# Inverting the scans' 64x64 unit triangular blocks on their diagonal 32x32 blocks

## The reference

```python
def gdn_chunked(q, k, v, g, beta, s0):
    cs = GDN_CHUNK                                   # 64
    ...
    tri_strict = jnp.tril(jnp.ones((cs, cs), bool), -1)
    a_mat = jnp.where(tri_strict, jnp.einsum('nbhid,nbhjd->nbhij', kb, kc) * decay, 0.0)
    eye = jnp.eye(cs, dtype=jnp.float32)
    t_mat = lax.linalg.triangular_solve(eye + a_mat, jnp.broadcast_to(eye, a_mat.shape),
                                        left_side=True, lower=True, unit_diagonal=True)
    u = jnp.einsum('nbhij,nbhjd->nbhid', t_mat, vb)
    w = jnp.einsum('nbhij,nbhjd->nbhid', t_mat, kb * jnp.exp(gcum)[..., None])
    ...
```

## Time and profile before

| | us |
|---|---|
| median of 3 runs | 2939.48 |
| profiled execution | 2932.05 |
| its span | 2930.1 |
| PE busy in the span | 2539.1 (87%) |
| VectorE busy | 1476.8 (50%) |
| opener of each inversion | at 551.7, 741.7, 1292.8, 1420.6 |
| granted TensorE clock, mean | 0.92 of 2.4 GHz |

### The profile page before, as it was taken

One profiled execution on the slowest core, in us unless ns is written; L12 is line 12 of the kernel. 1 busy time (PEld: TensorE's weight loads), 2 busy tenths in 40 slices (PEclk: granted clock), 3 DMA queues, 4 the chain that ended last, 5 costly groups with the idle time before them and its releaser, 6 DMA issues. The chain is left out here.

```text
span 2930.1 us, 60098 instructions
## 1 busy us (share of the span) xinstructions
PE 2539.1 (87%) x25174; PEld 2106.5 (72%) x25174; DVE 1476.8 (50%) x2524; ACT 905.7 (31%) x1456; POOL 618.6 (21%) x323
## 2 busy tenths in 40 slices
PE   6956597786977798978988899999997898899998
PEld 3845485684855587768887788888885765688886
DVE  6787777536437764345553444134315455643242
ACT  3243224213124432522124322122214433432232
POOL 0010200110113121200103223222341300544444
PEclk9977697896988899989999999999998999899999
DMA  6521061000005342200004112111214200523232
GB/s 267 180 80 45 14 205 42 3 4 1 4 3 215 138 157 86 72 28 3 3 3 151 51 64 71 58 57 64 71 44 180 77 1 16 200 100 99 89 104 82
DMA packets 63139, 229.31 MB, mean 78 GB/s; under 512 B 6352, under 2 KB 12880, under 8 KB 60880
## 3 DMA queue, kind: packets, MB, share of 16 engines
q1 hardware_dynamic: 62928, 226.22, 22.3%
HBM read 211.52 MB, written 13.63 MB: 77 GB/s over the span
## 5 line engine op out<-in xcount | busy, mean ns | idle before, releaser
L2323 POOL TENSOR_TENSOR b_wl<-b_stage,b_wh 128x1024 fp32r<-128x1024 f32 (+1 forms) x72 | 186.7, 2593 | 477.1 <-ACT b_wh L2319 477.1
L2622 DVE SCALAR_TENSOR_TENSOR f_xr<-f_ps,cols,f_xr 128x511 f32<-128x511 f32 (+1 forms) x132 | 83.2, 658 | 326.2 <-ACT f_xr L2615 326.2
L2454 PE MATMUL f_ps<-h_h,b_wl 128*128 128x256 f32 (+1 forms) x672 | 226.3, 337 | 0.0
L2454 PE MATMUL f_ps<-h_h,b_wh 128*128 128x256 f32 (+1 forms) x672 | 226.1, 336 | 0.0
L2454 PE MATMUL f_ps<-h_l,b_wh 128*128 128x256 f32 (+1 forms) x672 | 225.8, 336 | 0.0
L2319 ACT ACTIVATE b_wh<-b_stage 128x1024 fp32r<-128x1024 f32 (+1 forms) x72 | 81.5, 1131 | 460.3 <-PE f_ps L2454 404.9
L2323 POOL TENSOR_TENSOR c_wl<-c_stage,c_wh 128x1024 fp32r<-128x1024 f32 (+1 forms) x68 | 176.6, 2597 | 221.6 <-ACT c_wh L2319 221.6
L2319 ACT ACTIVATE c_wh<-c_stage 128x1024 fp32r<-128x1024 f32 (+1 forms) x68 | 77.3, 1137 | 266.3 <-PE f_ps L2454 232.8
L2323 POOL TENSOR_TENSOR a_wl<-a_stage,a_wh 128x1024 fp32r<-128x1024 f32 x33 | 85.2, 2581 | 269.2 <-ACT a_wh L2319 269.2
L2454 PEld LDWEIGHTS f_ps<-h_h,b_wh 128*128 128x128 f32 x672 | 127.6, 190 | 13.7
L2454 PEld LDWEIGHTS f_ps<-h_h,b_wl 128*128 128x128 f32 x672 | 127.6, 190 | 13.2
(11 more groups left out here) (716 smaller groups left out, 6698.0 us busy)
## 6 DMA issues: line engine op xcount, KB each, us to landing
b_stage<-in_ffn_up SPq DMA_DIRECT2D x44, 512.0 KB, 3.2
c_stage<-in_ffn_up SPq DMA_DIRECT2D x44, 512.0 KB, 3.2
first_stage<-in_w_in SPq DMA_DIRECT2D x33, 512.0 KB, 3.7
a_stage<-in_ab_w SPq DMA_DIRECT2D x25, 512.0 KB, 3.6
p_hgrn_side_w<-in_ada_w SPq DMA_DIRECT2D x12, 1024.0 KB, 5.0
b_stage<-in_ffn_down SPq DMA_DIRECT2D x16, 704.0 KB, 4.1
c_stage<-in_ffn_down SPq DMA_DIRECT2D x16, 704.0 KB, 4.1
a_in_side_w<-in_ada_w SPq DMA_DIRECT2D x8, 1024.0 KB, 6.4
```

Of the source, the lines that this page charges most:

```text
L2323: self.nc.gpsimd.tensor_tensor(self.wl[:, slot, :w], self.stage[:, slot, :w], self.wh[:, slot, :w].bitcast(F32), ALU.subtract).then_inc(se ...
L2454: done = self.nc.tensor.matmul(out[s][:, :tn], w, x[:, k, t0:t0 + tn], start=k == 0 and n == 0, stop=k == job.kt - 1 and n == 2)
L2622: nc.vector.scalar_tensor_tensor(out, b[:, :n - 1], self.tap(part, 0, i), out, ALU.mult, ALU.add).then_inc(self.before_ok[part], 1)
```

## The change

The stage works on the diagonal 32x32 blocks up to level 4: a tile of 128 partitions has four of them, one in each strip of 32 rows, and strip r uses the array's rows and columns of strip r. Weights are 32x32, and the moving operand has 16 columns. Level 5 joins the two 32x32 blocks of a chunk by two products with 32 moving columns.

In the order in which it runs:
- Start. ScalarE fills `both` (the new `upper` and `lower` in one buffer) with identities. PE turns and copies the blocks straight from the input (two matmuls a block and strip), and VectorE copies the neighbours of the diagonal out of PSUM with a predicated copy. GpSimd's two masked products are gone.
- Levels 1 to 4 as before, on blocks of 32; `cx` has one buffer for each level, all zeroed at the start, so that no memset waits for a product.
- Level 5. PE copies both near blocks of a pair into its bank (four matmuls with 256 moving columns), zeroes the empty part (two more, with zeros), and computes the corner product into a bank of its own. VectorE (pairs 0, 1, 4) or ScalarE (pairs 2, 3) carries it to `cx`, PE multiplies it by `upper` into the far corner, and the other one of the two engines copies the whole 64x64 blocks out.
- The masks `masks32` (line 344) become `masks16`, and a small fourth array of masks is loaded at the program's start. `masks64` is cut to 9 entries where the scans load it.

The diff, cut to its core:

```diff
+B = 32
...
-            sp.dma_start(rows[:, :, :], d["masks32"]).then_inc(loaded, 16)
-            sp.wait_ge(loaded, 48)
+            sp.dma_start(rows[:, :, :], d["masks16"]).then_inc(loaded, 16)
+            sp.dma_start(near[:, :, :], d["masks_near"]).then_inc(loaded, 16)
+            sp.wait_ge(loaded, 64)
...
         def _(pool):
-            for lv in range(1, 3):
-                nc.gpsimd.memset(cx[:, lv % 2], 0.0).then_inc(zeroed, 1)
-            for g in range(1, n_groups, 2):
-                nc.gpsimd.tensor_tensor(upper[:, group(g)], lt(g), spread(m64[:, M64[f"level0_{d}"], :], 1, 4), ALU.mult
-                                        ).then_inc(masked, 1)
-            for lv in range(1, 4):
-                for p in range(n_pairs):
-                    pool.wait_ge(product2, at_step[p, lv] + 1)
-                    nc.gpsimd.memset(cx[:, lv % 2, tiles(p)], 0.0).then_inc(zeroed, 1)
+            nc.gpsimd.memset(zeros[:, :], 0.0).then_inc(zeroed, 1)
+            for lv in range(1, 5):
+                nc.gpsimd.memset(cx[:, lv - 1], 0.0).then_inc(zeroed, 1)
 
         def _(dve):
...
+                dve.wait_ge(turned, p + 1)
+                got = banks[p][:, :].rearrange("p (e x) -> p e x", e=2)[:, :, :B * n].rearrange("p e (a q) -> p e a q", q=B)
+                dve.wait_ge(ones_in, p + 1)
+                nc.vector.copy_predicated(both[:, :, tiles(p), :], spread(near, 2, n).bitcast(mybir.dt.int32), got).then_inc(kept, 1)
...
+                        if p in halves[0]:
+                            dve.wait_ge(product1, at_step[min(p | 1, n_pairs - 1), 5] + 1)
+                            for c in range(2):
+                                rows = rows32(2 * c + 1 - d)
+                                ins = nc.vector.tensor_copy(cx[rows, 0, tiles(p)],
+                                                            corner_of(p)[rows, :].rearrange("p (a q) -> p a q", q=B))
+                            ins.then_inc(corner_read[0], 1)
...
             for p, pair in enumerate(pairs):
-                pe.wait_ge(first, 2 * p + 2)
-                for g, a, at, tile, half in each(p):
-                    done = nc.tensor.matmul(banks[p][half, at * C:(at + 1) * C], upper[half, tile, :], ident[half, :],
-                                            start=True, stop=True)
+                for g, a, at, tile, rows, cols in each(p):
+                    eye, block_lt = ident[rows, cols], lt(g)[rows, a, cols]
+                    nc.tensor.matmul(banks[p][rows, at * B:at * B + B], eye, block_lt, start=True, stop=True)
+                    done = nc.tensor.matmul(banks[p][rows, 256 + at * B:256 + at * B + B], block_lt, eye, start=True, stop=True)
                 done.then_inc(turned, 1)
-            for lv in range(1, 6):
+            for lv in range(1, 5):
...
-                    for g, a, at, tile, half in each(p):
-                        done = nc.tensor.matmul(banks[p][half, at * 32:at * 32 + 32], lt(g)[half, a, :], one(lower[half, tile, :], lv, d),
-                                                start=True, stop=True)
+                    for g, a, at, tile, rows, cols in each(p):
+                        done = nc.tensor.matmul(banks[p][rows, at * 16:at * 16 + 16], lt(g)[rows, a, cols],
+                                                one(lower[rows, tile, :], lv, d), start=True, stop=True)
...
+            near_cols, far_cols = cols32(d), cols32(1 - d)
+            pe.wait_ge(zeroed, 1)
+            for p, pair in enumerate(pairs):
+                pe.wait_ge(added, at_step[p, 4] + 1)
+                for r in range(4):
+                    rows, cols = rows32(r), cols32(r % 2)
+                    nc.tensor.matmul(wide(p)[rows, :, cols], ident[rows, cols], upper[rows, tiles(p), :], start=True, stop=True)
+                for c in range(2):
+                    rows = rows32(2 * c + 1 - d)
+                    nc.tensor.matmul(wide(p)[rows, :, near_cols], ident[rows, far_cols],
+                                     spread(zeros[rows, :], 1, 4 * len(pair)), start=True, stop=True)
+                for g, a, at, tile, inner, outer in corners(p):
+                    at = B * at
+                    done = nc.tensor.matmul(corner_of(p)[outer, at:at + B], lt(g)[inner, a, far_cols],
+                                            lower[inner, tile, :], start=True, stop=True)
+                done.then_inc(product1, 1)
+            for p, pair in enumerate(pairs):
+                e = p // 2 % 2
+                pe.wait_ge(corner_read[e], halves[e].index(p) + 1)
+                for g, a, at, tile, inner, outer in corners(p):
+                    done = nc.tensor.matmul(wide(p)[inner, at, far_cols], cx[outer, 0, tile, :], upper[outer, tile, :],
+                                            start=True, stop=True)
+                done.then_inc(product2, 1)
```

More of the change, by code:

```diff
@@ L341, in masks64, with masks16, masks_near, rows32 @@
     return np.ascontiguousarray(np.stack([m[name].astype(np.float32) for name in M64], 1))
-def masks32():
-    j, q = (np.arange(P) % C)[:, None], np.arange(C // 2)[None, :]
+def masks16():
+    j, q = (np.arange(P) % B)[:, None], np.arange(B // 2)[None, :]
     m = {}
     for d in range(2):
-        for lv in range(1, 6):
+        for lv in range(1, 5):
             s = 1 << lv
             m[f"row{lv}_{d}"] = (j // (2 * s) == q // s) & (j // s % 2 == 1 - d)
-    return np.ascontiguousarray(np.stack([m[name].astype(np.float32) for name in M32], 1))
+    return np.ascontiguousarray(np.stack([m[name].astype(np.float32) for name in M16], 1))
+def masks_near():
+    j, q = (np.arange(P) % B)[:, None], np.arange(B)[None, :]
+    pair, out = j // 2 == q // 2, []
+    for d in range(2):
+        for part in range(2):
+            before = j < q if d == part else j > q
+            out.append(pair & before)
+    out.append(j == q)
+    return np.ascontiguousarray(np.stack(out, 1).astype(np.float32))
+def rows32(r):
+    return slice(B * r, B * r + B)
+def cols32(h):
+    return slice(B * h, B * h + B)
 def rows64(c):
@@ L455, in setup @@
     ones = keep("ones", [P, P])
-    rows = keep("maskrow", [P, len(M32), C // 2])
+    rows, near = keep("maskrow", [P, len(M16), B // 2]), keep("near", [P, 5, B])
     with Stage(nc, "setup") as st:
@@ L1251, in inverses64 @@
     at_step = {key: n for n, key in enumerate(steps)}
-    m64, ident = t["mask64"], t["mask64"][:, M64["ident"], :]
+    ident = t["mask64"][:, M64["ident"], :]
+    near = t["near"][:, 2 * d:2 * d + 2, :]
     with Stage(nc, name) as st:
[L1254 to L1260, removed]
+        both = st.sbuf("both", [P, 2, 4 * n_groups, B])
+        upper, lower = both[:, 0], both[:, 1]
+        cx = st.sbuf("cx", [P, 4, 4 * n_groups, B])
+        zeros = st.sbuf("zeros", [P, B])
+        zeroed, ones_in, turned, kept, carried = (st.sem(s) for s in ("zeroed", "ones_in", "turned", "kept", "carried"))
+        product1, picked, product2, added, joined = (
+            st.sem(s) for s in ("product1", "picked", "product2", "added", "joined"))
+        corner_read = [st.sem(f"corner_read{e}") for e in range(2)]
+        halves = [[p for p in range(n_pairs) if p // 2 % 2 == e] for e in range(2)]
+        banks, corner = st.banks("b", n_pairs), st.banks("corner", (n_pairs + 1) // 2)
         if beside is not None:
@@ L1301, in _ @@
+            for lv in range(1, 5):
+                nc.gpsimd.memset(cx[:, lv - 1], 0.0).then_inc(zeroed, 1)
         @block.vector
         def _(dve):
-            own = Chain(dve, first)
             for p, pair in enumerate(pairs):
[L1305 to L1310, removed]
+                n = 4 * len(pair)
+                dve.wait_ge(turned, p + 1)
+                got = banks[p][:, :].rearrange("p (e x) -> p e x", e=2)[:, :, :B * n].rearrange("p e (a q) -> p e a q", q=B)
+                dve.wait_ge(ones_in, p + 1)
+                nc.vector.copy_predicated(both[:, :, tiles(p), :], spread(near, 2, n).bitcast(mybir.dt.int32), got).then_inc(kept, 1)
@@ L1342, in _ @@
                     beside.on_act(act, n)
[L1343 to L1347, removed]
+            for p in halves[1]:
+                act.wait_ge(product1, at_step[min(p | 1, n_pairs - 1), 5] + 1)
+                for c in range(2):
+                    rows = rows32(2 * c + 1 - d)
+                    ins = nc.scalar.activation(cx[rows, 0, tiles(p)],
+                                               corner_of(p)[rows, :].rearrange("p (a q) -> p a q", q=B), ACT.Copy)
+                ins.then_inc(corner_read[1], 1)
+            for p in halves[0]:
+                act.wait_ge(product2, at_step[p, 5] + 1)
+                for j, g in enumerate(pairs[p]):
+                    nc.scalar.activation(xt(g), wide(p)[:, 4 * j:4 * j + 4, :], ACT.Copy).then_inc(carried, 1)
         @block.tensor
```

72 lines of the change are left out of this document (41 added, 31 removed).

## The result

| | before | after |
|---|---|---|
| median of the runs (4 each) | 2939.35 us | 3110.91 us |
| ratio, with its 95% interval | | 1.059 [1.0577, 1.0603] |
| span of the profiled execution | 2930.1 us | 3109.6 us |
| the four inversions, opener to the next stage's first matmul | 73.1 + 72.1 + 57.7 + 57.1 = 260.0 us | 126.6 + 128.6 + 86.6 + 91.5 = 433.3 us |
| the rest of the span | 2670 us | 2676 us |

The change made the kernel 172 us slower by the medians (180 us by the two spans), where I had forecast 86 us faster. The four inversions take 173 us more.

The account below looks back on a forecast made before the run. TensorE (PE) was taken as the inversions' bound, at 58.3 ns a slot. Terms 77.2 + 16 - 0.3 - 6 - 0.4 = 86.5 us less gave 2853 us, own range 2832 to 2870, chance 0.53.

Parts of the forecast that it names:

- Levels 1 to 4: All four inversions: 2880 slots falling from 58.3 to 31.5 ns each, 77.2 us less.
- the slot of 31.5 ns: Estimated time for each active array tile to take one record with 32 weight columns; ends 26.7 and 58.3 ns.
- break-even: Slot length at which the change gains nothing: 55.6 ns, reached at a packet interval of 1.85 us.
- The front stage: Stage with 64x64 weights on four tiles: 8 records with loads in 0.115 us, twice the inversion's rate, cited against slow supply.
- rival 1: All levels: the slot doesn't shrink, through a hidden fixed cost or instruction supply; 2950 us, or 2957 at 60 ns; chance 0.18.
- Start of the stage: Before level 1: PE turns the input right behind the opener, 16 us less together; bounds 0 and 21.
- Last level: Corner products keep 480 slots at a shorter slot, plus new near-block copies by matmul: 0.3 us more; bounds -3 and +6.
- New VectorE waits in gdn: In gdn levels shorter PE work no longer covers VectorE: 6 us more; bounds 0 and 12.
- Setup DMA: Program start: one more DMA issue on SP, 0.4 us more, or nothing if its landing is hidden.
- Rival 2: A partial gain: PE can't issue eight loads and matmuls in 31.5 ns; slot 44 ns, 2897 us; chance 0.20.
- Rival 3: The clock falls to 1.2 GHz because half the cells are active; slot 56 ns, 2941 us, no change; chance 0.09.
- The rule of 60 cycles a matmul: Skill's fixed cost against small moving sizes: per pass it gives 2950 us; per record, 25 ns, it leaves the forecast.

## Why the prediction was wrong

**The bound.** That PE's slot limits the kernel before (58.3 ns) held: there PE never pauses in a level. But it takes its 256 instructions in 256 x 14.6 = 3.73 us, where the supply brings them in 3.46 to 3.7. The cover was 1 to 7%, and the whole change lived on the other side of it.

**Levels 1 to 4: the step that failed is the slot of 31.5 ns**, and behind it the sentence on the supply, "if packets follow each other closely this just holds; if a gap as long as the packet lies between them the slot is 60 ns". The array would have delivered: a burst of 32 slots takes 1.11 us at 2.4 GHz with 32 columns, 34.7 ns a slot, inside my 29 to 36 (with 16 columns no burst of the levels ran at 2.4 GHz, so that one isn't shown). But the interval of packets is not 1.0 or 2.0 us; it is 3.6. I had read how long a packet takes (1.0 us) and took that for the supply, with a guess for the gap. The half-sized packet that I counted with the six of the earlier trace rows belongs to another queue (q14), so a packet is 256 records and not 266. At 3.61 us the slot is 113 ns, and 2880 slots cost 2880 x (113 - 58.3) = 157 us more; measured 148.

The number stood in the trace of before, in the stage behind the inversion, where I hadn't read it (windows, then timeline):
```profile
638.89:641.20 2.31, 2.30 (x128) 2.22 (x128) 0.84 (x3) 0.88 (x3) 0.00 (x0) 1.00 0.02 7
641.20:642.30 1.10, 0.10 (x2) 0.00 (x0) 0.93 (x4) 0.00 (x0) 0.00 (x0) 1.00 0.00 0
```
```profile
642.35 0.98 PE L1425 MATMUL rwkv_chunks_m<-rw_al,rw_late 64*64 64x128 f32 x14 [1.05 <-issue]
```
256 instructions, a pause that nothing explains, and 3.45 us from one start to the next. My break-even was an interval of 1.85 us, so this row alone would have turned the forecast round.

**The front stage misled.** It runs 8 matmul records with their 8 loads in 0.115 us, 7.2 ns each, but in runs of 160 records with waits of 0.4 us between them. From 537 to 551 us it takes 804 records in 14 us, 17 ns each, slower than the supply's 14.1. It showed what PE can take in a burst, not what it can go on taking. The prediction used it as the argument against rival 1.

**Start of the stage.** The order did what was said: the first turn starts right behind the opener (1.9 us instead of 5.9). The 1152 instructions of the turns in place of 288 then took four intervals, and 16 us of gain became 15 of loss. On 64x64 tiles, with a quarter of those instructions, the step holds: 6.1 us measured in rwkv for 6.8 forecast, 6.3 and 6.4 in gdn for 7.0, 17 us in all for 16. That its turns take as long as I had counted for the 32x32 ones (72 slots of 58.3 ns for 144 of 31.5) is chance.

**Last level.** 0.3 forecast, 9.9 measured. Its 696 instructions in rwkv (576 for the corners, 120 for the wide copies) are 2.7 intervals of the supply. With 64 columns in the levels, where the clock is at 1.00 in three of the four last levels, the part takes 41.3 us for 44.2 here and 34.3 before. So some 3 us can be put down to the clock, and some 7 stay where it is full; these I haven't taken apart.

**New VectorE waits in gdn.** None came. PE's idle time in the gdn levels is "issue", and VectorE waits for PE. The term had been worked out for a PE twice as fast.

**Setup DMA.** Not to be told: the first inversion starts at 556.9 after and at 551.7 before, but in the kernels with the old setup it starts anywhere from 551.5 to 560.4.

**The rivals.** Rival 1 (0.18) named the mechanism, the place and the sign, and priced it at 10 to 17 us instead of 172, because its own term had no row. Rival 2 (a slot of 44 ns, because PE can't issue faster) had no say in the time; the bursts at 2.4 GHz have 34.7 ns in the levels and 39.7 in the turns (256 instructions in 1.27 us), between my estimate and this one. Rival 3 (the clock falls) happened as well; under a supply of 14.1 ns an instruction it costs next to nothing in the levels, since a burst of 1.70 us and one of 1.11 both wait for the same packet. Its slot of 56 ns at 1.2 GHz came near the 53 measured inside a burst.

**The rule that I had drawn on.** The trace speaks against the eight blocks that the Trainium skill, "Runtime: NRT & Kernel Launch", Instruction fetch mechanics, gives PE as a buffer. In the kernel with doubled products PE took 293 instructions from 561.2 to 568.3, and next to none in the 4.5 us before; at 14.1 ns each the queue could have brought some 800 in that time. It brought one packet between 552.5 and 569.2, and PE still paused after 305 more. In the changed kernel the first pause came after 327. Less than two blocks stood ready each time. The rule of 60 cycles a matmul (the Trainium skill, "TensorEngine Tiling (Array Packing)", Instruction Overhead) neither helped nor hurt. Inside a burst at 1.2 GHz 16 and 32 columns do take the same 1.69 us, which agrees with it, but the pause behind the burst hides what it would cost.

## What to carry to other kernels

Count instructions as well as work: on this core PE got 256 in 3.5 to 3.7 us on the average, some 14 ns each, and an f32 matmul needs four of them, so a plan that makes each matmul cheaper and twice as many gains nothing once a matmul comes more often than every 56 ns. A pause of PE that waits for "issue" after 256 instructions, with one instruction packet for each burst, is the mark of that limit; look for it in every stage of the kernel before, not only in the one that changes. When a term hangs on an interval, read a start-to-start distance under load; how long one transfer takes says little about how often they come.

## What the runs showed of the hardware that I had not expected

- The supply has a nearly fixed interval: 3.46 us at the shortest, often 3.73 or 4.0 in steps of 0.27, the same whether PE is at 1.2 or 2.4 GHz and whether the burst takes 1.11, 1.27, 1.70 or 1.87 us. The packet itself moves for 0.9 to 1.4 us of it; a burst starts 1.2 to 1.6 us after a packet has landed, and the next packet starts only 1.0 to 1.5 us after the burst has.
- The clock is low beside supply pauses in some kernels and not in others: with 16 moving columns it stayed at 1.2 GHz for all the levels and with 32 for all those of rwkv (in gdn it went up and down), with 64 columns it was at 2.4 GHz in nearly all, though PE paused some 1.5 us in every 3.46 there.
- A NOP between matmuls costs PE 34 ns at 2.4 GHz (92 instead of 58.3 ns for the four instructions around it).
- A slightly slower stream of 64x64 products loses the clock too: with the NOPs the kernel before ran nearly all its levels at 1.2 GHz, 106.6 ns a product instead of 58.3, and was 178 us slower with no pause in their levels.
